# Conditioning sums folded on VectorE, maxima rows by DMA, panel copies and affine passes reordered, the last output halves in two queues

## What is computed

```python
c_act = silu(c)
for layer in range(2):
    mod = c_act @ ada_w[layer] + ada_b[layer]          # 1024 x 6144
    sh_m, sc_m, g_m, sh_f, sc_f, g_f = split(mod, 6)
    hm = x * (1 + sc_m) + sh_m
    y = gla_mlstm_mixer(hm, ...) if layer == 0 else sb_dilated_mixer(hm, ...)
    x = layer_norm(ALPHA * x + (1 + g_m) * y, ln_g[layer, 0], ln_b[layer, 0])
    hf = x * (1 + sc_f) + sh_f
    yf = (silu(hf @ w1) * (hf @ w3)) @ w2
    x = layer_norm(ALPHA * x + (1 + g_f) * yf, ln_g[layer, 1], ln_b[layer, 1])
```

## Time and profile before

| | |
|---|---|
| Median of 3 runs | 1331.03 us (1327.98 to 1331.96) |
| Profiled execution | 1334.0 us |
| Its span in the trace | 1332.2 us |
| Mean granted clock of TensorE | 0.991 |
| TensorE busy | 1293.3 us, 97% |
| VectorE busy | 642.1 us, 48% |
| GpSimd busy | 505.8 us, 38% |
| ScalarE busy | 475.4 us, 36% |

### The profile page before, as it was taken

The page is one execution under the profiler, slowest core; times in us unless marked ns, Lnnn a source line. Parts: engine busy times, 40 slices in busy tenths (PEclk is TensorE's granted clock), DMA queues, the critical chain, the costliest instruction groups (busy, mean ns, idle before and its releaser), DMA issues.

```text
span 1332.2 us, 16978 instructions
## 1 busy us (share of the span) xinstructions
PE 1293.3 (97%) x6486; PEld 1079.4 (81%) x6486; DVE 642.1 (48%) x851; ACT 475.4 (36%) x683; POOL 505.8 (38%) x207
## 2 busy tenths in 40 slices
PE   7999999999999999999999899999999999999996
PEld 6878877789888888888887677888898888888884
DVE  5489746868543534410457766667781011110005
ACT  3443344633313232211342456535442222322222
POOL 0243322423535353544234223322354444444444
PEclk9999999999999999999999899999999999999998
DMA  9971636630655554873136522231122322234312
GB/s 330 187 157 66 221 107 116 223 109 20 234 188 190 185 193 161 271 121 96 63 116 237 150 79 64 75 116 48 53 100 92 104 94 94 94 96 146 102 52 63
DMA packets 93538, 173.61 MB, mean 130 GB/s; under 512 B 15735, under 2 KB 62087, under 8 KB 93356
## 3 DMA queue, kind: packets, MB, share of 16 engines
q1 hardware_dynamic: 90344, 169.43, 42.4%
q10 hardware_dynamic: 3140, 3.43, 1.0%
HBM read 170.68 MB, written 4.52 MB: 132 GB/s over the span
## 4 chain that ended last, share of the span: by engine, by line
PE 82%; DVE 7%; issue 5%; POOL 2%; DMA 1%; ACT 1%; SPq 0%; POOLq 0%; DVEq 0%; ACTq 0%
PE ps L1179 14%; PE ps L1180 14%; PE ps L1181 14%; PE ps L1211 6%; PE ps L1209 6%; PE ps L1210 6%; POOL w_lo L714 2%; PE ps L1613 1%; PE ps L1615 1%; PE ps L1614 1%; PE ps L1363 1%; PE ps L1317 1%; PE ps L1318 1%; PE ps L1319 1%; DMA ada_raw<-astream 1%
## 5 line engine op out<-in xcount | busy, mean ns | idle before, releaser
L714 POOL TENSOR_TENSOR w_lo<-raw,w_hi 128x1024 fp32r<-128x1024 f32 x191 | 475.1, 2495 | 784.6 <-ACT w_hi L772 780.7
L1179 PE MATMUL ps<-h_lo,w_hi 128*128 128x512 f32 (+2 forms) x1064 | 398.2, 374 | 3.4 <-DVE h_lo L2287 2.2
L1181 PE MATMUL ps<-h_hi,w_lo 128*128 128x512 f32 (+2 forms) x1064 | 394.7, 371 | 0.0
L1180 PE MATMUL ps<-h_hi,w_hi 128*128 128x512 f32 (+2 forms) x1064 | 394.7, 371 | 0.0
L772 ACT ACTIVATE w_hi<-raw 128x1024 fp32r<-128x1024 f32 x198 | 208.3, 1056 | 483.9 <-DMA raw<-wstream 159.2
L1179 PEld LDWEIGHTS ps<-h_lo,w_hi 128*128 128x128 f32 (+1 forms) x1064 | 201.3, 189 | 41.7 <-issue 4.9
L1181 PEld LDWEIGHTS ps<-h_hi,w_lo 128*128 128x128 f32 (+1 forms) x1064 | 201.1, 189 | 34.9
L1180 PEld LDWEIGHTS ps<-h_hi,w_hi 128*128 128x128 f32 (+1 forms) x1064 | 201.2, 189 | 33.5
L2406 DVE TENSOR_TENSOR tmp<-tmp,ps 128x512 f32<-128x512 f32 x44 | 30.1, 687 | 267.1 <-PE ps L1181 265.3
L1209 PE MATMUL ps<-w_hi,hid_lo 128*128 128x512 f32 x336 | 130.9, 390 | 0.0
L1211 PE MATMUL ps<-w_lo,hid_hi 128*128 128x512 f32 x336 | 130.7, 389 | 0.0
(11 more groups left out here) (297 smaller groups left out, 1620.0 us busy)
## 6 DMA issues: line engine op xcount, KB each, us to landing
raw<-wstream SPq DMA_DIRECT2D x205, 512.0 KB, 4.2
ada_raw<-astream SPq DMA_DIRECT2D x80, 512.0 KB, 4.4
ada_first<-astream SPq DMA_DIRECT2D x16, 256.0 KB, 6.8
ada_first<-astream SPq DMA_DIRECT2D x8, 512.0 KB, 10.3
ln_rows<-row_scratch SPq DMA_DIRECT2D x3, 1024.0 KB, 6.8
skew_scratch<-f_scratch ACTq DMA_DIRECT2D x1, 2304.0 KB
xa<-xT SPq DMA_DIRECT2D x4, 512.0 KB, 8.6
out<-xa SPq DMA_DIRECT2D x3, 512.0 KB, 3.5
```

The costliest lines, as they stand in the source:

```text
L714: nc.gpsimd.tensor_tensor(w_lo[:, slot, :], raw[:, slot % RAW, :], w_hi[:, slot, :].bitcast(F32), ALU.subtract).then_inc(sem("w_lo_ready"), 1)
L1179: pe.matmul(o, w_h, x_l, start=start, stop=False)
L1180: pe.matmul(o, w_h, x_h, start=False, stop=False)
L1181: return pe.matmul(o, w_l, x_h, start=False, stop=stop)
```

## The change

**Conditioning sums.** Behind the last slot of a block VectorE transposes `ada_acc` in squares of 32 by 32 and sums each square's rows, which leaves `ada_sum`, 128 x 32 (`ada_fold`; written out in the feed-forward loop at the second of four half steps, behind the accumulation). `ada_cols` is one product of it with a constant 128 x 128 matrix that holds a one where row and column agree modulo 32, and `mod_block` is four additions, each over 32 partitions and every fourth column.

**Maxima rows.** `neg_g` is stored to DRAM behind weight slot 20 in SyncE's queue, and read back spread over 128 partitions into `ng_rows`, two buffers in SBUF, behind slots 22 (two heads), 30 and 31. `neg_rows` is gone; `masked` and the exponentials read `ng_rows`.

**Order in layer 0.** The transposes of the mLSTM rows move behind the first slot of qkb0; the GLA scores alternate between the two row groups of a pair of heads; `ml_num(3)` comes ahead of `ada_cols(3)`; `ada_cols(4)` moves into the third block of the output projection, behind its fifth product. Block 2 folds behind the vb copies. Blocks 3 and 4 use their slots later. The low part of the last `out0` slot is made on VectorE, and ScalarE makes one more high part of `out0` ahead of the last four chunks. `modulation(0)` follows `residual(1)` instead of `residual(0)`.

**Order in layer 1.** In norm(1) the fourth slot's high part comes two chunks later. On VectorE two slots of block 11 and the first affine pass come ahead of the qc0 copy, two slots and the second pass ahead of the qc1 copy, and the last two passes and three slots between the kc0 and the vc copies; the loads of block 11 are spread over eleven weight slots instead of eight. `load_bias` moves to the end of the first round.

**The end.** The rows are copied into PSUM ahead of the third block's normalization instead of within it, `shift(2)` comes one instruction earlier, and ScalarE's queue issues the stores of the last two halves.

```diff
-C_IDENT, C_ONE, C_ZERO, C_NEG, C_DROP = 0, 128, 129, 130, 131
-C_N = 259
+C_IDENT, C_ONE, C_ZERO, C_NEG, C_DROP, C_SUM = 0, 128, 129, 130, 131, 259
+C_N = 387
...
+    c[:, C_SUM:C_SUM + P] = r[:, None] % 32 == r[None, :] % 32
...
+    ng_rows = ar("ng_rows", [P, 2, S], 20000)
+    ng_dram = nc.dram_tensor("ng_scratch", (4, S), F32, kind="Internal").ap()
...
-    ON_DVE = (HELD, SECOND)
+    ON_DVE = (OUT[0] + KC - 1, HELD, SECOND)
...
+    NG_OUT, NG_IN = 20, {22: (0, 1), 30: (2,), 31: (3,)}
...
+        def ng_in(h):
+            if h == 0:
+                sp.wait_ge(sem("ng_stored"), 16)
+            if h >= 2:
+                sp.wait_ge(sem("ml_w_ready"), h - 1)
+            sp.dma_start(ng_rows[:, h % 2, :], bass.AP(ng_dram.tensor, h * S, [[0, P], [1, S]])).then_inc(sem(f"ng_landed{h % 2}"), 16)
...
         for s in range(len(FIRST), s0):
             load(s)
+            for h in NG_IN.get(s, ()):
+                ng_in(h)
             for i in ADA_BESIDE.get(s, ()):
                 load_ada(i)
+            if s == NG_OUT:
+                sp.wait_ge(sem("row_step"), 4)
+                sp.dma_start(ng_dram, neg_g[:]).then_inc(sem("ng_stored"), 16)
...
-            if s < first + KC:
-                load_ada(KC * 11 + s - first)
+            for k in {0: (0,), 1: (1,), 3: (2,), 4: (3,), 6: (4, 5), 8: (6,), 10: (7,)}.get(s - first, ()):
+                load_ada(KC * 11 + k)
...
-        for b in range(2):
-            sp.wait_ge(sem("last_ready"), b + 1)
-            sp.dma_start(by_chunk(out[tile_of(TB - 1), b * S:(b + 1) * S]), xa[:, 4 * b:4 * b + 4, TB - 1, :]).then_inc(sem("stored"), 16)
...
-                                             ps[:, NG_BANK, (j + 1) * P:S], ACT.Exp, bias=bias)
+                                             ng_rows[:, h % 2, (j + 1) * P:S], ACT.Exp, bias=bias)
...
+        hi_until(out0 + 5)
...
-                if i == 3 and tb == 2:
-                    act.wait_ge(sem("in_rows"), 16)
-                    act.wait_ge(sem("r_ready"), TB * 3 + 2)
-                    for r in range(2):
-                        g = nc.scalar.activation(psf[:, 2 * r * S:2 * (r + 1) * S], rows_gb[:, r, :], ACT.Copy)
-                    g.then_inc(sem("rows_in_ps"), 1)
...
             if following is None:
                 normalize(1)
+                act.wait_ge(sem("in_rows"), 16)
+                act.wait_ge(sem("r_ready"), TB * 3 + 2)
+                for r in range(2):
+                    g = nc.scalar.activation(psf[:, 2 * r * S:2 * (r + 1) * S], rows_gb[:, r, :], ACT.Copy)
+                g.then_inc(sem("rows_in_ps"), 1)
                 normalize(2)
-                normalize(3)
+                std_of(3)
+                for b in range(2):
+                    act.wait_ge(sem("last_ready"), b + 1)
+                    act.dma_start(by_chunk(out[tile_of(TB - 1), b * S:(b + 1) * S]), xa[:, 4 * b:4 * b + 4, TB - 1, :]
+                                  ).then_inc(sem("stored"), 16)
...
-                if n == 5:
+                if n == (7 if i == 1 else 5):
...
-            if p == 0:
-                act.wait_ge(sem("skewed"), 16)
-                act.wait_ge(sem("ada_step"), 12 * KC)
-                load_bias(act)
...
             hi_until(fill_slot(2 * p) + RING + 4)
+            if p == 0:
+                act.wait_ge(sem("skewed"), 16)
+                act.wait_ge(sem("ada_step"), 12 * KC)
+                load_bias(act)
...
-            pe.wait_ge(sem("ada_step"), KC * (blk + 1) if isinstance(blk, int) else KC * blk + KC)
-            for n in range(KC):
-                m = pe.matmul(ps[:, bank, n:n + 1], ada_acc[:, tile_of(n)], one_col, start=True, stop=True)
-            m.then_inc(sem("ada_cols"), 1)
+            pe.wait_ge(sem("ada_summed"), blk - 1)
+            pe.matmul(ps[:, bank, 0:32], cst[:, C_SUM:C_SUM + P], ada_sum[:], start=True, stop=True
+                      ).then_inc(sem("ada_cols"), 1)
...
+        panel("qkb0", KC, h_hi, h_lo, between=am_rows)
...
-        for h in range(4):
-            p, e = divmod(h, 2)
-            if h == 0:
-                pe.wait_ge(sem("kd_ready"), 2)
-            if h == 2:
-                pe.wait_ge(sem("em_ready"), 1)
+        for p in range(2):
+            pe.wait_ge(*((sem("em_ready"), 1) if p else (sem("kd_ready"), 2)))
             for tb in range(TB):
-                m = pe.matmul(ps[:, GLA_BANK[h], tile_of(tb)], k_in[64 * e:64 * e + 64, p, tile_of(tb)],
-                              q_in[64 * e:64 * e + 64, p, tile_of(tb)], start=True, stop=True)
-            m.then_inc(sem("gla_s_full"), 1)
+                for e in range(2):
+                    m = pe.matmul(ps[:, GLA_BANK[2 * p + e], tile_of(tb)], k_in[64 * e:64 * e + 64, p, tile_of(tb)],
+                                  q_in[64 * e:64 * e + 64, p, tile_of(tb)], start=True, stop=True)
+                    if tb == TB - 1:
+                        m.then_inc(sem("gla_s_full"), 1)
...
-            pe.matmul(ps[:, NG_BANK, :], mcon[0:4, M_SEL + h * P:M_SEL + (h + 1) * P], neg_g[:],
-                      start=True, stop=True).then_inc(sem("ng_full"), 1)
...
-        gate_units(3)
-        neg_rows(0)
-        gate_units(2)
+        gate_units(5)
         for h in range(3):
             ml_scores(h)
-            gate_units(2)
-            neg_rows(h + 1)
-            gate_units(1)
+            gate_units(3)
             ml_num(h)
             gate_units(3)
         ml_scores(3)
         gate_units(2)
-        pe.wait_ge(sem("ml_w_ready"), 4)
+        ml_num(3)
+        pe.wait_ge(sem("mod_ready"), 3)
         ada_cols(3)
-        ml_num(3)
         turn_in(0)
...
-        pe.wait_ge(sem("r_ready"), 1)
-        ada_cols(4, 1)
         pe.wait_ge(sem("h_ready"), H_BASE["cat0"] + KC)
         for k in range(KC):
             m = out_row(0, 2, k)
+            if k == 4:
+                pe.wait_ge(sem("r_ready"), 1)
+                ada_cols(4, 1)
...
-            V.tensor_tensor(mod[:, blk, :], ps[:, bank, 0:KC], vcol(V_ADAB + blk * KC, KC), ALU.add).then_inc(sem("mod_ready"), 1)
-
-        def ada_block(blk, before=True, ks=range(KC)):
+            for q in range(4):
+                r = slice(32 * q, 32 * q + 32)
+                i = V.tensor_tensor(mod[r, blk, :], ps[r, bank, q:32:4], vec[r, V_ADAB + blk * KC:V_ADAB + (blk + 1) * KC], ALU.add)
+            i.then_inc(sem("mod_ready"), 1)
+
+        def ada_fold(total):
+
+            dve.wait_ge(sem("ada_step"), total)
+            link(V.transpose(ada_acc[:], ada_acc[:]))
+            V.tensor_reduce(ada_sum[:], ada_acc[:].rearrange("q (b i) -> q b i", i=32), mybir.AxisListType.X, ALU.add
+                            ).then_inc(sem("ada_summed"), 1)
...
-        ada_block(2, False, range(4, KC))
+        ada_block(2, False, range(4, KC), False)
         v_blocks("vb")
+        ada_fold(3 * KC)
...
         weigh(3)
+        ada_fold(4 * KC)
         mod_block(3)
-        ada_block(4, False, range(0, 2))
...
-        ada_block(4, False, range(6, KC))
+        ada_block(4, False, range(4, 5))
+        lo_of_slot(OUT[0] + KC - 1)
+        ada_block(4, False, range(5, KC))
...
+                    if b == 0:
+                        shift(2)
...
-                if i == 0 and tb == 0:
+                if i == 0 and tb == 1:
...
+                    if u == 1:
+                        dve.wait_ge(sem("ada_step"), 8 * it + 48)
+                        V.transpose(ada_acc[:], ada_acc[:]).then_inc(sem("ada_turned"), 1)
+                        dve.wait_ge(sem("ada_turned"), it + 1)
+                        V.tensor_reduce(ada_sum[:], ada_acc[:].rearrange("q (b i) -> q b i", i=32), mybir.AxisListType.X, ALU.add
+                                        ).then_inc(sem("ada_summed"), 1)
...
+        V.memset(vd[:, :, :, 1, :], 1.0)
+        ada_block(11, False, range(2), False)
+        rest1((0,))
         qk_panel("qc0")
+        ada_block(11, False, range(2, 4), False)
+        rest1((1,))
         qk_panel("qc1")
+        ada_block(11, False, range(4, 5), False)
         dve.wait_ge(sem("f_full"), 1)
         V.tensor_copy(f_rows[:], ps[0:4, 4:7, 0:F_LEN]).then_inc(sem("f_ready"), 1)
         mod_block(10)
-        ada_block(11, False, range(4))
         qk_panel("kc0")
-        ada_block(11, False, range(4, KC))
-        rest1()
-        V.memset(vd[:, :, :, 1, :], 1.0)
+        rest1((2,))
+        ada_block(11, False, range(5, 7), False)
+        rest1((3,))
+        ada_block(11, False, range(7, KC), False)
+        ada_fold(12 * KC)
         v_blocks("vc")
         mod_block(11)
         gate_col(3)
```

65 lines of the change are left out of this document (34 added, 31 removed).

## The result

The changed kernel takes 1309.2 us, median of four runs (1307.87 to 1311.62), beside 1331.07 for the kernel before on the same chips: the ratio is 0.9841, with a 95% interval from 0.9825 to 0.9857. The forecast was 1300.0, from 1291 to 1309. The sign was right, the median lies 0.2 us above the range, and 9 us of the forecast gain did not come.

A forecast was written before the change was run, and what follows sets the result against it. TensorE, busy 97% of the span, was taken as the bound: only fewer or cheaper instructions or shorter waits help. Terms sum to 31.1 us off the profiled 1334.0, giving 1302.9, as a median 1300; range 1291 to 1309.

The forecast's parts named there:

- Conditioning sums: Column sums of blocks 2 to 11: 16 TensorE instructions become two, 1.68 us becomes 0.28 a block; 14.0 us gained.
- Maxima rows: Four `neg_rows` leave TensorE, 1.05 us each, 4.2 us gained; the DMAs replacing them priced at nothing.
- the low clock at 173 us: Low-clock stretch behind block 2's column sums, 1.6 us lost before; half, 0.8 us, taken as gained.
- Row transposes and scores: mLSTM row transposes no longer wait, 1.1 us gained; 32 GLA score products alternate row groups, 0.6 us gained.
- Output projection of layer 0: Split waits in `out_row` go, 2.0 us gained; later block 4 costs 0.9 (0 to 3) at `turn(0, 0)`; net 1.1.
- First half of norm(1): An earlier `h_lo` subtraction, no longer slowed by a GpSimd split, starts `residual(3)` and the second turn 1.9 us earlier.
- Projections of layer 1: VectorE passes collide with GpSimd splits: new 2.2 us wait at `kc0`; the 1.3 wait ahead of vc becomes 2.0.
- The vc copies: In layer 1 the 4.6 us wait for the vc copy goes, and the low clock behind it, 2.3 us.
- The first attention round: Moving `load_bias` lets VectorE's scans fall from 6.52 towards 4.86 us; 1.3 us gained, 0 if they stay.
- The end: Earlier row copy and `shift(2)`, own queue for the last halves' stores: 2.1 us gained (1.4 to 2.6).
- The second, that new waits take more: Rival: low clock behind new waits, nothing gained at 173, more wait at `turn(0, 0)`; 7.5 us less, 1307.4; chance 0.18.
- three signs of being wrong: Fold over 5 us; SP's queue holding raw slots up behind the maxima; `residual(0)` late by more than 8 us.

The follow-up runs named there:

- the base: The changed kernel with 128 unused bytes per partition ahead of the large shared SBUF area, which holds the feed-forward's hidden rows; 1302.94 us.
- the kernel with 64 bytes: The changed kernel with 64 unused bytes ahead of the large shared SBUF area; 1306.92 us in a single run.

## Why the prediction was right and wrong

**What bounds the kernel** was read rightly, but not to its end. "Fewer or cheaper TensorE instructions" was taken as a matter of counts. The pace of the products was taken over from the kernel before as a constant; it is not one.

**Conditioning sums**: right, and a little better than forecast: 1.57 us a block instead of 1.4, since the new product takes 0.14 us of the path and not 0.28. The fold's 2.5 us were 2.47. The step that failed is one that was not written: the change was costed by its instructions alone, and its 640 bytes of new tiles were costed at nothing without being named. They took 6.4 us back in the traces, at 0.2324 us a product in the second down projection instead of 0.2267, and 6.3 between the medians (1309.2 and 1302.9). With that one term undone the kernel lies at 1302.94, inside the range, 2.9 us above the forecast. That it comes so near is in part luck: layer 0's end was 5 us worse than its terms, and the other stages together some 6 better.

**Maxima rows and the low clock at 173 us**: the four products went (4.2 forecast; with the sums of block 3 and a wait of 0.5 that went too, 7.0 measured against 5.6), no queue held anything up, and the low stretch went whole: 1.6, of which the forecast had taken half.

**Row transposes and scores**: 1.9 beside 1.7.

**Output projection of layer 0**: here the forecast failed in a second place. The 2.0 us of waits for the splits went, as said, and block 4 came late by about the 6 us that were said. But the early split, which was seen only as a gain, meets a gating product of VectorE with two SBUF operands and holds it for 1.7 us, and TensorE waits 2.4. And `modulation(0)`, which was costed at nothing, now falls between the splits of the feed-forward's first slots: 4.7 us for two operations of 0.16. The step that failed is the cover of a moved step: of the 0.9 us (0 to 3) at `turn(0, 0)` none came there, but 2.9 us at the first `tmp`, and a low clock behind it, 1.6. The run with `modulation(0)` ahead of the splits shows both operations at 0.16 and 0.17 us and that wait gone. The forecast had used the same rule, that the passes wait for splits, twice in layer 1 and not here.

**First half of norm(1)**: 1.9 forecast, 2.2 measured, with the late low part that was named (0.9 us of wait).

**Projections of layer 1**: the mechanism was right. The timeline of VectorE in the changed kernel:

```profile
673.36 3.23 DVE L1950 SCALAR_TENSOR_TENSOR ada_acc<-ada_raw,c_act,ada_acc 128x1024 f32<-128x1024 f32 x1
676.51 3.42 DVE L2393 TENSOR_TENSOR xa<-xa,ln_rows 128x1024 f32<-128x1024 f32 x1
679.96 3.27 DVE L2394 TENSOR_TENSOR xa<-xa,ln_rows 128x1024 f32<-128x1024 f32 x1
683.16 0.68 DVE L2490 TENSOR_SCALAR qc<-ps 128x512 f32<-128x512 f32 x1
```

Accumulation and passes take 3.2 to 3.4 us each, as the one of the earlier trace rows, the copy is late, and TensorE waits 1.5 us (2.2 forecast). The second wait did not grow to 2.0 but fell to 0.8. So this stage is 2.2 us above its forecast. The vc copies gave 7.5 (6.9). The first attention round gave 0.6 and not 1.3. Its scans take 4.84 us as forecast, but the reason given is not borne out: with `load_bias` at its old place they take 4.51. That `load_bias` had to move for the rest to hold was not seen.

**The end**: 2.2 beside 2.1. The last halves are issued by ScalarE's queue right behind the first half's addition, where the earlier trace rows has SyncE's queue at 1326.49 and later:

```profile
1300.02 1.41 DVE L2388 SCALAR_TENSOR_TENSOR xa<-xa,rstd,ps 128x512 f32<-128x512 f32 x2
...
1300.80 1.08 ACTq L1024 DMA_DIRECT2D out<-xa  x2
```

**The rivals.** The second, that new waits take more, gave the nearest time, 1307.4, but for the wrong reason: two of its terms came (2 us in norm(0), a low clock behind a wait), one did not (173 us), and the largest single loss, the 6.4 us of the down projections, was in none of the rivals. Their conditions all lay in the order of instructions; none lay in the data's place. Nor did one of the three signs of being wrong come: the fold takes 2.47 us, no queue held slots up behind the maxima, and `residual(0)` was not 8 us late.

## What to carry to other kernels

A change that adds a tile moves every tile allocated behind it, and that is part of its cost: compare the count of equal products in a window of a stage that the change does not touch. Here the two operands of a product, the streamed and the loaded one, should lie at the same place modulo 256 bytes. When a step is moved, ask for each of its instructions with two SBUF operands, the smallest too, whether a GpSimd instruction is under way at its new place; it costs the rest of that instruction, not its own length. And a wait that is taken away may have been the cover of another one: the move of `load_bias`, entered at 1.3 us in the forecast, was worth 7.7.

## What was not expected of the hardware

A TensorE that is 100% busy at a granted clock of 1.00 ran 2.5% slower, at 0.2324 us a product of 512 columns against 0.2267, by the place of its two SBUF operands against each other: 0 bytes modulo 256 apart is fast, 128 is slow, and 64 is in between (0.2289) or slow (0.234), by which of the two lies above the other.

The low clock behind a wait is not certain, and the length of the wait doesn't decide it. In the wait for `tmp`, TensorE ran at 0.50 behind 2.9 us in the changed kernel and at 1.00 behind 2.8 us in the base, but at 0.50 again behind 2.7 us in the kernel with 64 bytes. Behind the wait of 1.5 us in front of the first kc product, five of the nine traces that have it show the low clock; the base is one of them, the changed kernel is not. At either place, first the changed kernel, then the base:

```profile
284.00:285.00 1.00, 1.00 (x6) 1.00 (x6) 1.00 (x4) 0.63 (x3) 0.00 (x0) 0.50 0.00 0
```
```profile
284.00:285.00 1.00, 0.89 (x7) 0.89 (x8) 1.00 (x4) 0.59 (x2) 0.00 (x0) 1.00 0.00 0
```
```profile
685.00:686.00 1.00, 1.00 (x6) 0.83 (x5) 1.00 (x1) 0.00 (x0) 0.48 (x1) 1.00 0.00 0
```
```profile
682.00:683.00 1.00, 1.00 (x3) 0.72 (x3) 0.90 (x2) 0.00 (x0) 0.00 (x0) 0.50 0.00 0
```

In the changed kernel the low stretch costs 1.6 us. What decides whether it comes was not tried.
